# More dots of gathered expert rows ahead of the weights, with more gather buffers, six query low parts moved to GpSimd, and tree sums in the routing look-ups

## The reference, cut to what matters

```python
q = (hf @ w_query).reshape(T, 8, 2, 128)                 # 8 heads, two halves
s = einsum('thpd,pkd->thpk', q, sub_keys)                # 2 x 128 sub-keys
sv, si = top_k(s, 16)                                    # top 16 of each half
cand = sv[:, :, 0, :, None] + sv[:, :, 1, None, :]       # 256 pairs of a head
top_s, top_pos = top_k(cand, 16)
idx = take_along_axis(si0 * 128 + si1, top_pos)          # 16384 experts
g = softmax(top_s)
pre = einsum('td,thkd->thk', h, down[idx])               # a dot for each picked expert
out = einsum('thk,thkd->td', g * gelu(pre), up[idx])
```

## Time and profile before

| | |
|---|---|
| median of 3 runs | 1850.58 us (1848.67 to 1851.85) |
| the profiled execution's own time | 1846.17 us |
| its span, first to last instruction | 1844.4 us |
| first idx of block 0 (line 1590) | at 709.2 us |
| first down tile on PE (line 756) | at 718.2 us |
| first up tile on PE (line 769) | at 1248.5 us |
| dots made by then | 205 of 256 |
| last up tile on PE | at 1699.6 us |
| sums made by then | 167 of 256 |
| last sum (line 1678) | at 1821.8 us |

### The profile page before, as it was taken

How to read it: one execution, slowest core, us unless ns; L and a number is a source line. 1 busy time by engine, 2 the same in 40 slices (tenths; PEclk the granted TensorE clock), 3 DMA queues, 4 the chain that set the end, 5 groups by cost and what they waited for, 6 DMA issues and landing times.

```text
span 1844.4 us, 20738 instructions
## 1 busy us (share of the span) xinstructions
PE 1583.7 (86%) x7052; PEld 1170.7 (63%) x7052; DVE 1319.0 (72%) x2595; ACT 547.0 (30%) x1337; POOL 621.1 (34%) x527
## 2 busy tenths in 40 slices
PE   3998999988997979999999999999999989998000
PEld 2787877766876979888888888884444434443000
DVE  5766456667556598899875888886566566667998
ACT  2433234444623633111116888880000000000001
POOL 1000000000002512534454455456444464445772
PEclk8999999999998989999999999999999999999555
DMA  8423311123421536999998889889999999999995
GB/s 315 159 100 151 137 69 47 70 91 144 187 92 52 188 119 241 350 334 326 373 342 289 319 312 317 320 320 379 409 409 409 411 410 409 409 409 409 377 380 218
DMA packets 124232, 498.19 MB, mean 270 GB/s; under 512 B 13920, under 2 KB 14176, under 8 KB 113760
## 3 DMA queue, kind: packets, MB, share of 16 engines
q0 software_dynamic: 73728, 268.47, 38.5%
q1 hardware_dynamic: 50400, 228.41, 32.9%
HBM read 492.11 MB, written 4.72 MB: 269 GB/s over the span
## 4 chain that ended last, share of the span: by engine, by line
PE 34%; DVE 25%; DMA 25%; ACT 5%; issue 4%; POOL 3%; DVEq 3%; ACTq 1%; SPq 0%; POOLq 0%
DMA ring<-in_up,idx 16%; PE bank L756 9%; DVE accum L1678 8%; DMA ring<-in_down,idx 8%; PE bank L491 6%; PE bank L492 6%; PE bank L493 6%; DVE ring L1460 4%; POOL ring L1703 3%; PE bank L743 2%; DVE acc_ada L1118 2%; DMA raw<-in_ada 1%; ACT h2T L1037 1%; ACT h2T L1042 1%; ACT whi L791 1%
## 5 line engine op out<-in xcount | busy, mean ns | idle before, releaser
L756 PE MATMUL bank<-h2T,stream 128*128 128x256 f32 x2048 | 452.7, 380 | 2.3 <-ACTq L1071 2.3
L769 PE MATMUL bank<-stream,wmat 128*128 128x512 f32 x1024 | 443.5, 596 | 12.1 <-DMA stream<-in_up 8.2
L1703 POOL DMA_INDIRECT ring<-in_down,idx x256 | 306.0, 1195 | 374.5 <-DVE pre L1460 295.9
L1678 DVE SCALAR_TENSOR_TENSOR accum<-ring,share,accum 128x1024 f32<-128x1024 f32 x256 | 328.8, 1284 | 138.3 <-DMA ring<-in_up,idx 129.5
L756 PEld LDWEIGHTS bank<-h2T,stream 128*128 128x128 f32 x2048 | 386.8, 191 | 52.7 <-issue 2.7
L1460 DVE CUSTOM_DVE_ANT_0 ring<-ring,h2row 128x1024 f32<-128x1024 f32 x256 | 307.6, 1220 | 76.5 <-DMA ring<-in_down,idx 74.4
L769 PEld LDWEIGHTS bank<-stream,wmat 128*128 128x128 f32 x1024 | 196.0, 192 | 258.9 <-issue 245.8
L1703 POOL DMA_INDIRECT ring<-in_up,idx x256 | 263.8, 1031 | 211.8 <-DVE accum L1678 172.2
L491 PE MATMUL bank<-hT_hi,whi 128*128 128x512 f32 (+1 forms) x640 | 236.7, 370 | 29.5 <-DVE hT_lo L1171 12.3
L1712 POOL TENSOR_TENSOR wlo<-raw,whi 128x2048 fp32r<-128x2048 f32 x11 | 51.1, 4645 | 608.0 <-ACT whi L791 608.0
L492 PE MATMUL bank<-hT_lo,whi 128*128 128x512 f32 (+1 forms) x640 | 226.2, 353 | 0.0
(11 more groups left out here) (211 smaller groups left out, 1633.7 us busy)
## 6 DMA issues: line engine op xcount, KB each, us to landing
stream<-in_downT SPq DMA_DIRECT2D x128, 512.0 KB, 5.8
stream<-in_up SPq DMA_DIRECT2D x128, 512.0 KB, 6.8
raw<-in_ada SPq DMA_DIRECT2D x24, 1024.0 KB, 5.3
raw<-in_w_query SPq DMA_DIRECT2D x16, 1024.0 KB, 4.8
raw<-in_w_xp SPq DMA_DIRECT2D x4, 1024.0 KB, 6.7
raw<-in_w_gateA SPq DMA_DIRECT2D x4, 1024.0 KB, 4.8
raw<-in_w_branchP SPq DMA_DIRECT2D x4, 1024.0 KB, 4.8
raw<-in_w_q SPq DMA_DIRECT2D x4, 1024.0 KB, 4.8
```

The costliest lines, as they stand in the source:

```text
L756: last = pe.matmul(bank[:, 4 + i % 2, 0:DT], stream[:, i % RING, k * P:(k + 1) * P], h2T[:, k, GB * P:S], start=(k == 0), stop=(k == KT - 1))
L769: last = pe.matmul(bank[:, 2 * tb + half, :], wmat[:, i, tb * P:(tb + 1) * P], stream[:, (ET + i) % RING, half * S:(half + 1) * S], start= ...
L1678: dve.scalar_tensor_tensor(accum[:, b, :], ring[slot][:, :], share[:, b, k:k + 1], accum[:, b, :], ALU.mult, ALU.add).then_inc(sum_done, 1)
L1703: pool.indirect_dma_start(out=ring[slot][:, :], out_offset=None, in_=table, in_offset=bass.IndirectOffsetOnAxis(ap=idx[:, b, k:k + 1], axi ...
```

## The change

It does seven things.

1. The gathers of the down pass get seven buffers for the first 125 dots (`EARLY_SLOTS`), five until `w_ready` (`STEP_SLOTS`), and the last dots and the whole up pass get nine. The new ones lie where the rotary tables lay (`rope_at`) and at 132 and 136 KB. The buffer of a gather is the one of its set that was used least recently.
2. `ROUTE_PER_DOT` goes from 1.4 to 0.985, and the dots of the routing are no longer limited to the first 128: 113 dots in the routing instead of 89, 125 instead of 101 before the spreading stretch.
3. In the spreading stretch each step makes two dots, and a third where the step's number is a multiple of 3 and it has one quad: 13 more dots, so that 242 are made at `w_ready` instead of 205. 14 are left instead of 51.
4. POOL makes all 16 query chunks' low parts. DVE makes none, and its stage2(0) runs without fillers. POOL makes 14 before its first gather (`POOL_FIRST`), the 15th after the second gather and the 16th after the fourth (`POOL_MORE = 2`).
5. The reduction of 16 in the look-ups becomes four additions in place, over 8, 4, 2 and 1 of the 16 elements: bf16, the last one into the result.
6. The four one-hots of a quad (four `tensor_scalar` of 128 x 128) become one `tensor_tensor` of 128 x 512 with broadcast operands.
7. `gel_tmp` and `o_junk` are placed elsewhere.

```diff
-URING = 8
+URING = 9
+EARLY_SLOTS = (0, 1, 2, 3, 8, 9, 10)
+STEP_SLOTS = (0, 1, 2, 3, 8)
+MORE_DOTS = 3
-LATE_DOTS = 205
-ROUTE_PER_WLO = 4.5
-POOLED = 10
-ROUTE_PER_DOT = 1.4
+EARLY_DOTS = 125
+LATE_DOTS = 242
+POOLED = 16
+POOL_FIRST = 14
+POOL_MORE = 2
+ROUTE_PER_DOT = 0.985
...
-            late = dots_before + RING
+            late = LATE_DOTS + len(STEP_SLOTS)
             for g in range(GB * P):
-                slot = g % RING if g < late else (g - late + late % RING) % URING
+                slots = EARLY_SLOTS if g < EARLY_DOTS else STEP_SLOTS if g < late else range(URING)
+                slot = min(slots, key=lambda n: at_slot[n][-1] if at_slot[n] else -1)
...
                 while credit[0] >= ROUTE_PER_DOT:
                     credit[0] -= ROUTE_PER_DOT
-                    dots(1, P)
+                    dots(1)
...
-                    fill(2.4)
-                    dve.tensor_reduce(dst.rearrange("p (a b) -> p a b", a=PH), onehot, AX.X, ALU.add)
+                    fill(1.2)
+                    for w in (8, 4, 2):
+                        dve.tensor_tensor(onehot[:, :, :, 0:w], onehot[:, :, :, 0:w], onehot[:, :, :, w:2 * w], ALU.add)
+                        dve.drain()
+                    fill(1.2)
+                    dve.tensor_tensor(dst.rearrange("p (a b) -> p a b", a=PH).unsqueeze(3), onehot[:, :, :, 0:1],
+                                      onehot[:, :, :, 1:2], ALU.add)
                     dve.drain()
-                    fill(2.4)
...
-            stage2(0, fill_lows)
-            while split[0] < len(CHUNKS):
-                follow(split[0])
-                split[0] += 1
+            stage2(0, nothing)
             stage2(1, fill)
...
-            dots(DOTS_EXP, P)
+            dots(DOTS_EXP)
...
-                for n in range(4):
-                    t = t0 + n
-                    last = dve.tensor_scalar(h2T[:, 4 * par + n, 0:P], iota, ijT[:, b, 1, t:t + 1], None, ALU.is_equal)
-                last.then_inc(oh_ready, 1)
+                dve.tensor_tensor(h2T[:, 4 * par:4 * par + 4, 0:P], iota.unsqueeze(1).broadcast_to([P, 4, P]),
+                                  ijT[:, b, 1, t0:t0 + 4].unsqueeze(2).broadcast_to([P, 4, P]),
+                                  ALU.is_equal).then_inc(oh_ready, 1)
...
-                dots(STEP_DOTS)
+                dots(STEP_DOTS + (i % MORE_DOTS == 0 and len(quads_at(i)) == 1))
...
-            for n in POOL_CHUNKS:
+            def wlo_make(n):
+
                 if n:
                     pool.wait_ge(lo_ready, n)
                 pool.wait_ge(hi_ready, n + 1)
...
-            pool.wait_ge(x1_stored, 16)
+            for n in POOL_CHUNKS:
+                if n < QUERY + POOL_FIRST:
+                    wlo_make(n)
             for g in range(GB * P):
                 b, k = g // P, g % P
                 if k == 0:
                     pool.wait_ge(idx_ready, b + 1)
+                if g == 0:
+                    pool.wait_ge(x1_stored, 16)
                 if down_prior[g] is not None:
                     pool.wait_ge(dot_done, down_prior[g] + 1)
-                elif down_slot[g] >= RING:
+                elif RING <= down_slot[g] < 8:
                     pool.wait_ge(gmm, DT // 4)
                 gather(down, b, k, down_slot[g])
+                late = QUERY + POOL_FIRST + (g + 1) // POOL_MORE - 1
+                if (g + 1) % POOL_MORE == 0 and late < len(CHUNKS):
+                    wlo_make(late)
```

More of the change, by code:

```diff
@@ L218, in layer @@
         subk = small("subk", [P, 2, NKEYS])
+        o_junk = small("o_junk", [P, P])
+        gel_tmp = place("gel_tmp", [P, 2, DT], f32, low[0] - 2)
         rope_at = low[0]
         rope_cos = small("rope_cos", [P, S])
-        gel_tmp = place("gel_tmp", [P, 2, DT], f32, rope_at)
         rope_sin = small("rope_sin", [P, S])
@@ L236, in layer @@
         o_root = small("o_root", [P, HEADS * TB])
-        o_junk = small("o_junk", [P, P])
         gain_o = small("gain_o", [P, HEADS])
@@ L308, in layer @@
         stream = place("stream", [P, RING, D], f32, 164)
-        ring = [place(f"ring{n}", [P, D], f32, 180 + 4 * n if n < RING else 148 + 4 * (n - RING))
-                for n in range(URING)]
+        ring = [place(f"ring{n}", [P, D], f32, kb)
+                for n, kb in enumerate((180, 184, 188, 192, 148, 152, 156, 160, rope_at, 132, 136))]
         bias_row = place("bias_row", [P, D], f32, 197)
@@ L405, in layer @@
         w_ready = sem("w_ready")
-        ring_in = [sem(f"ring_in{n}") for n in range(URING)]
+        ring_in = [sem(f"ring_in{n}") for n in range(len(ring))]
         dot_done = sem("dot_done")
@@ L1088, in layer, with place_down @@
         down_slot, down_round, down_prior = [], [], []
-        at_slot = [[] for _ in range(URING)]
-        def place_down(dots_before):
-            late = dots_before + RING
+        at_slot = [[] for _ in ring]
+        def place_down():
+            late = LATE_DOTS + len(STEP_SLOTS)
             for g in range(GB * P):
-                slot = g % RING if g < late else (g - late + late % RING) % URING
+                slots = EARLY_SLOTS if g < EARLY_DOTS else STEP_SLOTS if g < late else range(URING)
+                slot = min(slots, key=lambda n: at_slot[n][-1] if at_slot[n] else -1)
                 down_prior.append(at_slot[slot][-1] if at_slot[slot] else None)
@@ L1099, in place_down @@
                 at_slot[slot].append(g)
-        place_down(LATE_DOTS)
+        place_down()
         @block.vector
@@ L1465, in _ @@
             credit = [0.0]
[L1466 to L1471, removed]
-                    follow(split[0])
-                    split[0] += 1
-                    split[1] = 0.0
             def fill(us):
@@ L1621, in _ @@
                 softmax(b)
-            dots(DOTS_PICK, P)
+            dots(DOTS_PICK)
             def one_hots(q):
@@ L1649, in weigh @@
                                   ALU.mult).then_inc(weighed, 1)
+            assert done[0] == EARLY_DOTS, done
             for q in quads_at(SPREAD_AT):
```

## The result

The changed kernel takes 1817.45 us (median of 4 runs, 1816.33 to 1819.12), against 1849.62 for the kernel before on the same chip: ratio 0.9824, 95% interval 0.9805 to 0.9844. The profiled execution took 1818.49 us, 27.7 less than the one of before.

What follows compares the result with a forecast made beforehand. PE bounds the down stretch, PE and DMA the up stretch, DVE the tail. Terms: -51.0 + 15.7 + 2 + 1 = -32.3 us, first up tile (T) at 1267, 1813.9 profiled, median 1818; 8-in-10 range 1798 to 1838.

Steps and rivals of the forecast that it cites:

- Term 1: DVE's tail after the up tiles: 242 dots instead of 205 before the first up tile, 37 x 1.378 = -51.0 us.
- Term 2: stage2(0) on DVE: no low parts and cheaper trees, less 8.7 us of POOL lock; idx at 702.8, only 6.4 us earlier.
- Term 3: First gathers between POOL's last low parts: 12.4 us of waits against some 4; first down tile at 727, not counting by itself.
- Term 4: DVE's routes, which ACT awaits at tile 66: they end at 968.5, moving the first up tile by +15.7 us.
- Term 5: Spreading stretch: 13 third dots mostly taken up by DVE's slack, cost 2 us, plus 1 at the last steps.
- Little lock: POOL and DVE get by each other: idx at 694, gain 47 to 41 us, 1804 to 1810; chance 0.23.
- Gathers short: DVE waits for rows in three-dot steps and later routing: first up tile 10 to 20 us later, 1829 to 1839; chance 0.20.
- slower: Down tiles plus gathers already at the DMA's ceiling of 328 GB/s: end 15 us later, about 1865; chance 0.04.

## Why the prediction was right

**Term 1, the tail.** Right in mechanism: 54 sums are left, 1.378 us apart, as these 11 show, (15.06 - 1.285)/10:

```profile
1720.93 15.06 DVE L1675 SCALAR_TENSOR_TENSOR accum<-ring,share,accum 128x1024 f32<-128x1024 f32 x11
```

The tail shrank by 48.8 us and the up stretch grew by 1.0: -47.8 instead of -51.0. Two rows fewer passed in the up stretch (216, not 218). The run without third dots and the one without 24 dots bear out the price of a row: 15.7 us for 13 and 33 for 24, so 1.2 and 1.38 us each. That the ninth buffer adds nothing was shown too.

**Term 2, the first indices.** idx came at 705.4, 2.6 later than said. 1.8 us of it arose in a part that the change does not touch: PE's ninth query chunk started at 654.69 instead of 652.92. Counted from there, idx came 5.6 us earlier than before the change, where the prediction had 6.4. The tree was cheaper than the reduction, but by 0.2 us, not 0.4:

```profile
703.23 1.66 DVE L1583 TENSOR_TENSOR hot<-hot 128x1024 bf16<-128x1024 bf16 x3
704.96 0.39 DVE L1586 TENSOR_TENSOR rowij<-hot 128x128 f32<-128x128 bf16 x1
705.42 0.29 DVE L1590 SCALAR_TENSOR_TENSOR idx<-rowij 128x128 int32<-128x128 f32 x1
```

From 703.23 to 705.42 are 2.19 us, against 2.40 for the reduction with its drain (704.38 to 706.78 before). The lock cost twice 4.4 us, where the sum had 4.2 and 4.5, at the two places named. Only the instruction held was another: a cast, with one SBUF input, just ahead of the pairs. The rule of the Trainium skill, page "SBUF — State Buffer", section "Who interferes with whom", names casts, which can run in a mode that uses both ports, beside instructions with two inputs. The trace agrees: a cast was held for 4.4 us and a dot for 2.3. Whether these casts ran in that mode no row shows.

**Term 3, the start of the gathers.** As said: gathers 0 and 1, then a low part, then 2 and 3, then a low part; PE's gap was 16.4 us. The first down tile came at 729.9 instead of 727. From the end of idx to the fourth dot, waits and lock took 11.4 us (3.42 + 2.31 + 1.95 + 2.80 + 0.90), against 12.4 in the sum. That the late first down tile did not count was shown by the run with all 16 low parts first: PE's first down tile 20 us earlier, T the same.

**Term 4, the end of the routes.** 972.4 instead of 968.5; from the end of idx 266.7 us against 265.7. The parts were off against each other: waits for gathers were 7.6 us and two dots were held for 5.1 more, together 12.7 instead of 15.4, and the rest, 254.0 us, was 3.7 more than 250.3.

**Term 5, the spreading stretch.** 3 us in the sum. The first up tile moved 20.0 us, the routes' end 19.5, so it cost about 0.5. The run without third dots puts their price at 1.2.

**The sum.** T +20.0 instead of +18.7, tail and up stretch -47.8 instead of -51.0: the span fell by 27.8 us, not by 32.3. In the medians the fall is 32.2 us, so the closeness of 1818 to 1817.45 is in part luck. The prediction took the profiled execution to lie 4.4 us below the median, as before the change; it lay 1.0 above. The terms by themselves were 4.5 us too good.

**The rivals.** Little lock: refuted by the two casts. Gathers short, and slower: refuted by 385 GB/s over 242 us of the routing, where I had asked whether 336 or 350 could be passed; DVE waited for gathers 7.6 us there and 6.6 in the spreading stretch.

The prediction saw PE wait for the routes, but took that as a price to be paid. PE's 10.3 us at tile 68 could be had by moving one number.

No run takes out the tree sums by themselves, or the five buffers of the spreading stretch; of the trees the rows show the 0.2 us each.

## What to carry to other kernels

Find the stretch in which one engine works alone at the end, and price moved work by that engine's time there (1.378 us), not by what it cost where it stood (2.06 us). An extra on an engine's list costs what the wait that it lengthens costs: 13 dots in a stretch where DVE had idle time cost 1.2 us, 24 in a stretch that PE waited for cost 10, and that wait could be put off. Before work is moved from DVE to POOL, look what DVE does meanwhile: of the four low parts that newly ran beside the routing ahead of idx, two cost it nothing and two held it for nearly their whole length.

## What the runs showed of the hardware

A POOL `tensor_tensor` of 4.6 us held a 0.2 us cast of DVE for 4.4 us, and the profile shows it as busy time of the cast. It held a DVE instruction with two inputs too (5.47 us instead of 1.23), and beside DVE's search for the top 16 it cost nothing. The other way round, an indirect DMA that POOL issued 0.10 us after DVE had begun a `tensor_tensor` of 2.29 us took 3.15 us instead of 1.13. Gathers and streamed tiles together moved 385 GB/s over 242 us with seven buffers, and 349 over 266 us of the same work with four. Seven buffers instead of four were worth 25 us in the routing, and nine instead of eight nothing in the up stretch.
